# A one-core hybrid decoder layer: one weight split moved on two engines, and the order of the gated-embedding tail rewritten

## The chip, the core and the metric

The kernel runs on one NeuronCore of a Trainium2 chip. The metric is the time of one execution in microseconds (us) of device time; lower is better. TensorE does the matmuls into PSUM, VectorE and ScalarE the elementwise work, GpSimd one-column arithmetic and the transfers that add, and SyncE issues most other transfers.

## The reference

One decoder layer on 512 tokens of width 1024, in fp32: attention and a gated mixer, a squared-ReLU MLP, and at the end an input embedding `p` gated per layer. Only that last part, with the product in front of it, is touched:

```
gate = jax.nn.sigmoid(jnp.einsum('bsd,de->bse', h, w_ple_gate[i]) + b_ple_gate[i])
ple = jnp.einsum('bsp,pd->bsd', p[i], w_ple[i]) * gate
h = h + rms_norm(ple, ple_post_g[i])
```

`h` is 512 x 1024, `w_ple_gate` 1024 x 1024. `rms_norm` divides each token's row by the root of its mean square and multiplies by a gain row.

## The kernel before

Five instruction streams are written out by hand, one per engine, and tied by semaphores; each engine works through its stream strictly in order. An fp32 product is made from three matmuls: every operand is split into a high part, which ScalarE rounds off (a "hi" copy), and a low part, which VectorE subtracts (a "lo" split); TensorE then multiplies high by high, low by high, high by low (lines 2694, 2698, 2699). Tokens are handled in four tiles of 128 rows, t = 0 to 3.

**The gate product.** `h @ w_ple_gate` is cut into 2 x 2 blocks and made by seven block products (a Strassen scheme), each for two token tiles j = 0, 1. `GATE_PRODUCTS` gives TensorE's order: (0,0), (0,1), (1,0), (1,1), (2,0), (3,0), (2,1), (4,0), (3,1), (5,0), (4,1), (6,0), (5,1), (6,1), written (block, j); a product is 12 matmuls of 512 columns, and the last one is made in two halves of 256. The weights of the seven blocks are GATE_11, GATE_21, GATE_T1, GATE_T2, GATE_T3, GATE_T4, GATE_22. The T blocks are sums of weight blocks. GpSimd's queue makes them with adding transfers into `raw_second` or `raw` (`add_gate`, line 2467), in two parts each. A part of T4 is added to the same place as the same part of T2, so its transfer waits until VectorE's lo split of that part of T2 is done. In a split weight `gate_split_hi` (ACT L2120) reads the raw sum, then `gate_split_lo` (DVE L1355). The tokens' side needs the turned hidden state: TensorE turns a tile of `h` by four small matmuls per half (`turn_h2`, L2749) into PSUM bank 6 or 7, and ScalarE copies it out (`h2_copy_raw`, L2160, into `h2T_a` or `h2T_b`; `h2_split_hi`, L2166). There are eight such halves, i = 0 to 7, and halves 6 and 7 use the banks of halves 4 and 5. `seed_e` (L2198) writes the bias into two banks, `gate_copy` (L2209) copies a product's result to where it is added to. `h2_sum` (L1403) makes sums of blocks of the hidden state, which are split in the same way (L2182, L1408).

**The tail.** The gated rows are made in nine pieces (`GATE_TILES`): 0 = (t0, left), 1 = (t1, left), 2 = (t2, right), 3 = (t2, left), 4 = (t3, right), 5 = (t0, right), 6 = (t3, left), 7 and 8 = the two quarters of (t1, right). For each there is `sigmoid(i)` (ACT L2220, or L2217 for pieces 2 and 4), `gate_ple(i)`, a multiply with the embedding (DVE L1440), and `square_ple(i)`, which sums squares (ACT L1596). GpSimd adds a token tile's sums, one column each (L2506, L2517), takes the power -1/2 (L2519) and so gives the tile's `rstd`. Tiles are finished in the order 2, 0, 3, 1. For t = 2 and 0 (`ADDED_IN_OUT`) VectorE scales the gated rows by rstd and gain (L1464), and GpSimd issues an adding store into `out` (L2527), on top of `h`, which is stored there earlier. For t = 3 and 1 VectorE multiplies by the gain (`gain_ple`, L1452) and adds rstd times that to `h` (L1473), and SyncE stores each piece (L2679). For the very last piece, 8, GpSimd writes the root of the partial sum into an extra column beside the piece (L2510), so that the last square gives the whole sum. GpSimd's loop takes a whole tile at a time: partial sums, rstd, then the wait for VectorE's scaling and the adding store, and then the next tile.

Of the kernel before, what the change touches and what calls it, by code (L numbers as in the profile page):

```python
# [39 lines left out]
P = 128  # L40
D = 1024
# [274 lines left out]
def hymba_layer(nc, x, xT, pT, weights, columns, rope, ws, rows, out):  # L316
# [6 lines left out]
    with ExitStack() as ctx:  # L323
# [158 lines left out]
        ple_tmp = stat[:, 56:59]  # L482
# [260 lines left out]
        def _(dve):  # L743
# [712 lines left out]
            def add_ple(t):  # L1456

                tiles = gate_tiles_of(t)
                if t in ADDED_IN_OUT:
                    dve.wait_ge(pl_rstd, TOKENS_DONE.index(t) + 1)  # L1460
                    for i in tiles:
                        dve.wait_ge(pl_gated, i + 1)
                        cut = slice(GATE_TILES[i][1], GATE_TILES[i][1] + GATE_TILES[i][2])
                        nc.vector.scalar_tensor_tensor(out=ple_of(t)[:, cut], in0=acc[:, t, cut],  # L1464
                                                       scalar=rstd_pl[:, t:t + 1], in1=ple_gain[:, cut],
                                                       op0=ALU.mult, op1=ALU.mult).then_inc(out_ready, 1)
                    return
                gain_ple(tiles[-1])
                dve.wait_ge(pl_rstd, TOKENS_DONE.index(t) + 1)
                dve.wait_ge(pl_gained, GAINED.index(tiles[-1]) + 1)  # L1470
                for i in tiles:
                    cut = slice(GATE_TILES[i][1], GATE_TILES[i][1] + GATE_TILES[i][2])
                    nc.vector.scalar_tensor_tensor(out=h[:, t, cut], in0=ple_of(t)[:, cut],  # L1473
                                                   scalar=rstd_pl[:, t:t + 1], in1=h[:, t, cut],
                                                   op0=ALU.mult, op1=ALU.add).then_inc(out_ready, 1)
# [27 lines left out]
            gate_split_lo(GATE_T2, 1)  # L1503
# [3 lines left out]
            h2_sum_split_lo(OF_E, 0)  # L1507
            h2_sum_split_lo(OF_S2, 0)
# [26 lines left out]
            add_ple(2)  # L1535
# [15 lines left out]
        def _(act):  # L1551
# [702 lines left out]
            gate_split_hi(GATE_T2, 1)  # L2254
            seed_e(0)
            seed_e(1)
# [3 lines left out]
            h2_split_hi(5)  # L2260
            h2_sum_split_hi(OF_E, 0)
            h2_sum_split_hi(OF_S2, 0)
# [27 lines left out]
            for i in range(4, len(GATE_TILES)):  # L2290
                sigmoid(i)
                square_ple(i)
# [5 lines left out]
        def _(pool):  # L2298
# [201 lines left out]
            for n, t in enumerate(TOKENS_DONE):  # L2500
                *before, last_tile = gate_tiles_of(t)
                total = D * EPS
                for place_in_row, i in enumerate(before):
                    partial = ple_tmp[:, place_in_row:place_in_row + 1]
                    pool.wait_ge(pl_squared, i + 1)
                    after(nc.gpsimd.tensor_scalar(partial, ss_pl[:, i:i + 1], total, None, ALU.add))  # L2506
                    total = partial
                if last_tile == LAST_GATED:

                    nc.gpsimd.tensor_tensor(last_gated[:, width_of(LAST_GATED):], total, plus_half, ALU.pow  # L2510
                                            ).then_inc(root_ready, 1)
                    pool.wait_ge(pl_squared, last_tile + 1)
                    mean = ss_pl[:, last_tile:last_tile + 1]
                else:
                    pool.wait_ge(pl_squared, last_tile + 1)
# [759 lines left out]
```

## Time and profile before

| what | value |
|---|---|
| median of 3 runs (lowest, highest) | 585.18 us (585.04, 585.37) |
| the profiled execution's own time | 586.4 us |
| its span, first to last instruction | 584.7 us |
| granted TensorE clock, mean of the span | 0.991 of full speed |
| TensorE busy, share of the span | 97% |
| VectorE, ScalarE, GpSimd busy | 86%, 64%, 20% |

The profiled execution is one more execution than the three timed ones. Its span leaves out 1.7 us before the first and behind the last instruction. Rows of the trace give the start from the span's beginning in us, the duration, and in brackets how long the engine had been idle and what released it.

### The profile page before, as it was taken

The numbers are of one execution on the slowest core, as the hardware profiler recorded it, in microseconds if no ns is written. First come the engines' busy times: TensorE is split into PE (matmuls) and PEld (weight loads), VectorE is DVE, ScalarE is ACT, GpSimd is POOL, SyncE is SP. The second block draws the span as 40 slices with busy tenths as digits, with TensorE's granted clock in tenths as the row PEclk, the third lists the DMA queues.
The fourth block names the chain that finished last, engine by engine and source line by source line (L and its number), as shares of the span: only waits on it lengthen the run. The fifth ranks groups of instructions, "written<-read, shape, count | busy, mean of one in ns | idle before, by whom it ended". The sixth has DMA issues, their size and how long they took to land.

```text
span 584.7 us, 8927 instructions
## 1 busy us (share of the span) xinstructions
PE 569.1 (97%) x3364; PEld 496.0 (85%) x3364; DVE 501.1 (86%) x637; ACT 374.9 (64%) x595; POOL 114.2 (20%) x165
## 2 busy tenths in 40 slices
PE   9999999999999999999999999999999999999991
PEld 7888888888888888989999999999999999887881
DVE  5899895788676997999989999999899999787975
ACT  6886765785546646657665665666556655775862
POOL 0331536000104372101010011010100110123114
PEclk9999999999999999999999999999999999999996
DMA  8981008224003649377484592774754927877946
GB/s 270 372 309 62 0 5 321 73 72 143 3 1 109 243 173 298 78 228 188 89 256 106 143 253 44 246 161 90 242 121 112 281 40 214 242 234 141 288 128 140
DMA packets 28747, 95.30 MB, mean 163 GB/s; under 512 B 3232, under 2 KB 5664, under 8 KB 28320
## 3 DMA queue, kind: packets, MB, share of 16 engines
q1 hardware_dynamic: 20448, 67.64, 32.5%
q0 software_dynamic: 6672, 20.71, 20.6%
q10 hardware_dynamic: 1584, 6.37, 2.8%
q8 instruction: 27, 0.44, 0.3%
q14 instruction: 16, 0.13, 0.1%
HBM read 86.85 MB, written 7.34 MB: 161 GB/s over the span
## 4 chain that ended last, share of the span: by engine, by line
PE 77%; DVE 9%; DMA 6%; ACT 4%; POOL 2%; issue 2%; SPq 0%; DVEq 0%; ACTq 0%; POOLq 0%
PE psum L2694 24%; PE psum L2698 23%; PE psum L2699 23%; DMA ple_spill<-ple 2%; DVE up_lo L1078 2%; PE psum L2932 2%; DMA raw_second<-weights_dram 2%; PE psum L2912 1%; PE psum L2749 1%; DMA raw<-weights_dram 1%; ACT junk_late L1596 1%; DVE ple L1172 1%; DMA first_raw_a<-weights_dram 1%; PE psum L2763 1%; DVE t_lo L1223 1%
## 5 line engine op out<-in xcount | busy, mean ns | idle before, releaser
L2694 PE MATMUL psum<-t_hi,a_hi 128*128 128x512 f32 x216 | 85.0, 393 | 0.5 <-DVE acc L1282 0.5
L2698 PE MATMUL psum<-t_lo,a_hi 128*128 128x512 f32 x216 | 84.6, 392 | 0.0
L2699 PE MATMUL psum<-t_hi,a_lo 128*128 128x512 f32 x216 | 84.1, 389 | 0.0
L2694 PE MATMUL psum<-w_hi,actT_hi 128*128 128x512 f32 (+1 forms) x178 | 69.7, 392 | 0.0
L2699 PE MATMUL psum<-w_hi,actT_lo 128*128 128x512 f32 (+1 forms) x178 | 68.5, 385 | 0.0
L2698 PE MATMUL psum<-w_lo,actT_hi 128*128 128x512 f32 (+1 forms) x178 | 68.5, 385 | 0.0
L2698 PE MATMUL psum<-sum_lo,up_hi 128*128 128x256 f32 x224 | 63.4, 283 | 0.0
L2699 PE MATMUL psum<-sum_hi,up_lo 128*128 128x256 f32 x224 | 63.4, 283 | 0.0
L2694 PE MATMUL psum<-sum_hi,up_hi 128*128 128x256 f32 x224 | 63.2, 282 | 0.0
L2429 POOL DMA_DIRECT2D raw_x<-weights_dram x21 | 18.5, 882 | 216.1 <-DVE t_lo L1223 215.8
L2699 PE MATMUL psum<-actT_hi,up_lo 128*128 128x256 f32 (+1 forms) x200 | 60.0, 300 | 0.0
L2698 PE MATMUL psum<-actT_lo,up_hi 128*128 128x256 f32 (+1 forms) x200 | 60.0, 300 | 0.0
L2694 PE MATMUL psum<-actT_hi,up_hi 128*128 128x256 f32 (+1 forms) x200 | 59.9, 299 | 0.0
L1282 DVE TENSOR_TENSOR acc<-acc,psum 128x512 f32<-128x512 f32 x76 | 49.1, 681 | 1.8 <-PE psum L2699 1.8
L1078 DVE TENSOR_TENSOR up_lo<-raw,up_hi 128x1024 fp32r<-128x1024 f32 x37 | 46.8, 1264 | 2.6 <-ACT up_hi L1857 2.0
L2699 PEld LDWEIGHTS psum<-t_hi,a_lo 128*128 128x128 f32 x216 | 40.6, 188 | 8.9
L2694 PEld LDWEIGHTS psum<-t_hi,a_hi 128*128 128x128 f32 x216 | 40.7, 189 | 8.0 <-issue 0.8
L2698 PEld LDWEIGHTS psum<-t_lo,a_hi 128*128 128x128 f32 x216 | 40.7, 189 | 6.6
L2694 PEld LDWEIGHTS psum<-sum_hi,up_hi 128*128 128x128 f32 x224 | 42.9, 191 | 1.1
L2698 PEld LDWEIGHTS psum<-sum_lo,up_hi 128*128 128x128 f32 x224 | 42.9, 191 | 1.1
L2699 PEld LDWEIGHTS psum<-sum_hi,up_lo 128*128 128x128 f32 x224 | 42.9, 191 | 0.0
L2694 PEld LDWEIGHTS psum<-actT_hi,up_hi 128*128 128x128 f32 x200 | 38.2, 191 | 2.0
(298 smaller groups left out, 1453.7 us busy)
## 6 DMA issues: line engine op xcount, KB each, us to landing
raw<-weights_dram SPq DMA_DIRECT2D x40, 512.0 KB, 4.6
raw_o<-weights_dram SPq DMA_DIRECT2D x23, 512.0 KB, 4.4
raw_x<-weights_dram POOLq DMA_DIRECT2D x21, 512.0 KB, 5.5
raw_second<-weights_dram SPq DMA_DIRECT2D x16, 512.0 KB, 4.1
raw_x<-weights_dram SPq DMA_DIRECT2D x9, 512.0 KB, 6.2
qk_raw<-weights_dram SPq DMA_DIRECT2D x8, 512.0 KB, 6.7
raw_o<-weights_dram POOLq DMA_DIRECT2D x7, 512.0 KB, 6.9
raw_second<-weights_dram POOLq DMA_DIRECT2D x6, 512.0 KB, 7.7
```

The lines of the kernel that those rows point to most:

```text
L1078: nc.vector.tensor_tensor(up_lo[q % UP_SLOTS][:], block_source(step, j), up_hi[q % UP_SLOTS][:].bitcast(F32), ALU.subtract).then_inc(block ...
L1172: drained_by_dve(nc.vector.tensor_copy(ple[:, t, half * W:(half + 1) * W], psum[:, bank1["ple", i], :]), ("ple", i))
L1223: nc.vector.tensor_tensor(t_lo[n % T_RING][:], t_source(n), t_hi[n % T_RING][:].bitcast(F32), ALU.subtract).then_inc(t_lo_done, 1)
L1282: nc.vector.tensor_tensor(part, part, bank, how).then_inc(product_added, 1)
L1596: nc.scalar.activation(place_at[:, 0:source.shape[-1]], source, ACT.Square, scale=scale, accum_out=sums).then_inc(done, 1)
L2429: nc.gpsimd.dma_start(raw_x[step % 2][:], weights[down_in_stream(step, rows, half)], accum_op=ALU.add).then_inc(x_added, 16)
L2694: begin = nc.tensor.matmul(out, a_hi, b_hi, start=first, stop=False, skip_group_check=read_between)
L2698: nc.tensor.matmul(out, a_hi, b_lo, start=False, stop=False, skip_group_check=read_between)
L2699: return nc.tensor.matmul(out, a_lo, b_hi, start=False, stop=last, skip_group_check=read_between)
L2749: mm = nc.tensor.transpose(psum[:, banks[name], j * P:(j + 1) * P], source[:, j * P:(j + 1) * P], ident[:])
L2763: mm = nc.tensor.matmul(out, wsT[:, g, :], gv[:, :, g * GD:(g + 1) * GD], start=True, stop=True)
L2932: mm = nc.tensor.matmul(psum[s * DH:(s + 1) * DH, BANK_O, pair * P:(pair + 1) * P], v[:, k, head * DH:(head + 1) * DH], probsT_of[place_in ...
```

## The change

Nothing that is computed changes. (1) On ScalarE and VectorE the split of the second part of GATE_T2, which waits for an adding transfer, is moved behind the copies of the third token tile (t = 2, halves 4 and 5), the seeds and the first sum's split. (2) In the tail, ScalarE takes sigmoids 5, 6, 7 and 8 ahead of squares 4, 5, 6 and 7. (3) GpSimd makes the partial sums of squares as soon as a square is there, and the rstd of t = 3 ahead of the adding store of t = 0. (4) VectorE adds piece by piece, with the gains of pieces 6, 7 and 8 in other places. The scratch columns become one per tile, and SyncE's order of stores is written out with the same result for the pieces that it stores.

```diff
-        ple_tmp = stat[:, 56:59]
+        ple_partial, ple_mean = stat[:, 56:60], stat[:, 61:62]
...
             gate_split_lo(GATE_T2, 0)
-            gate_split_lo(GATE_T2, 1)
             h2_sum(OF_E, 0)
             h2_sum(OF_S2, 0)
             h2_sum(OF_S3, 0)
             h2_sum_split_lo(OF_E, 0)
+            gate_split_lo(GATE_T2, 1)
             h2_sum_split_lo(OF_S2, 0)
...
-            add_ple(2)
+            scale_ple(2)
             gate_ple(4)
             gate_ple(5)
             gain_ple(4)
-            add_ple(0)
+            scale_ple(0)
             gate_ple(6)
+            gain_ple(6)
             gate_ple(7)
-            add_ple(3)
             gain_ple(7)
+            add_ple(4)
             gate_ple(8)
+            add_ple(6)
+            gain_ple(8)
             add_ple(1)
+            add_ple(7)
+            add_ple(8)
...
             gate_copy(COPY_C11, 0)
-            gate_split_hi(GATE_T2, 1)
-            seed_e(0)
-            seed_e(1)
             gate_copy(COPY_C11, 1)
             h2_copy_raw(4)
             h2_copy_raw(5)
             h2_split_hi(5)
+            seed_e(0)
+            seed_e(1)
             h2_sum_split_hi(OF_E, 0)
+            gate_split_hi(GATE_T2, 1)
             h2_sum_split_hi(OF_S2, 0)
...
-            for i in range(4, len(GATE_TILES)):
-                sigmoid(i)
-                square_ple(i)
+            sigmoid(4)
+            sigmoid(5)
+            square_ple(4)
+            sigmoid(6)
+            square_ple(5)
+            sigmoid(7)
+            square_ple(6)
+            sigmoid(8)
+            square_ple(7)
+            square_ple(8)
...
+            partial_sum(0)
+            partial_sum(1)
+            partial_sum(2)
+            ple_rstd(2)
+            add_in_out(2)
+            partial_sum(4)
+            ple_rstd(0)
+            ple_rstd(3)
+            add_in_out(0)
+            partial_sum(7)
+            nc.gpsimd.tensor_tensor(last_gated[:, width_of(LAST_GATED):], ple_partial[:, 1:2], plus_half, ALU.pow
+                                    ).then_inc(root_ready, 1)
+            ple_rstd(1)
...
-            order = [i for t in TOKENS_DONE for i in gate_tiles_of(t)]
+            order = (2, 3, 0, 5, 4, 6, 1, 7, 8)
```

ScalarE's stream at the first place, before. `w_hi<-raw_second` is the split of T2's second part, `psum<-gate_bias_row` the two seeds, `h2T_b<-psum` the two copies of t = 2:

```order
L2209 ACTIVATE psum<-psum 128x512
L2120 ACTIVATE w_hi<-raw_second 128x1024
L2198 ACTIVATE psum<-gate_bias_row 128x512 x2
L2209 ACTIVATE psum<-psum 128x512
L2160 ACTIVATE h2T_b<-psum 128x4x128 x2
L2166 ACTIVATE actT_hi<-psum 128x4x128
L2182 ACTIVATE actT_hi<-gate_e 128x4x128
```

The same place with the change (three lines further down in the file):

```order
L2212 ACTIVATE psum<-psum 128x512 x2
L2163 ACTIVATE h2T_b<-psum 128x4x128 x2
L2169 ACTIVATE actT_hi<-psum 128x4x128
L2201 ACTIVATE psum<-gate_bias_row 128x512 x2
L2185 ACTIVATE actT_hi<-gate_e 128x4x128
L2123 ACTIVATE w_hi<-raw_second 128x1024
```

Seven instructions that stood behind the split now stand ahead of it.

GpSimd's stream at the end, before, from the adding store of t = 2 on. All of `stat<-stat` is one column wide; L2506 is a partial sum, L2517 the last addition of a tile, L2519 the power:

```order
L2527 DMA out_dram<-ple_late_b_147 128x1024
L2506 TENSOR_SCALAR stat_56<-stat_56 128x1
L2517 TENSOR_SCALAR stat_56<-stat_56 128x1
L2519 TENSOR_TENSOR stat_56<-stat_56 128x1
L2527 DMA out_dram<-ple_late_a_146 128x1024
L2506 TENSOR_SCALAR stat_56<-stat_56 128x1
L2517 TENSOR_SCALAR stat_56<-stat_56 128x1
L2519 TENSOR_TENSOR stat_56<-stat_56 128x1
L2506 TENSOR_SCALAR stat_56<-stat_56 128x1 x2
L2510 TENSOR_TENSOR last_gated_148<-stat_56 128x1
L2519 TENSOR_TENSOR stat_56<-stat_56 128x1
```

With the change the same stretch is (L2516, L2526, L2528, L2539 and L2551 answer to L2506, L2517, L2519, L2527 and L2510):

```order
L2539 DMA out_dram<-ple_late_b_147 128x1024
L2516 TENSOR_SCALAR stat_56<-stat_56 128x1
L2526 TENSOR_SCALAR stat_56<-stat_56 128x1
L2528 TENSOR_TENSOR stat_56<-stat_56 128x1
L2526 TENSOR_SCALAR stat_56<-stat_56 128x1
L2528 TENSOR_TENSOR stat_56<-stat_56 128x1
L2539 DMA out_dram<-ple_late_a_146 128x1024
L2516 TENSOR_SCALAR stat_56<-stat_56 128x1
L2551 TENSOR_TENSOR last_gated_148<-stat_56 128x1
L2528 TENSOR_TENSOR stat_56<-stat_56 128x1
```

The partial sum of piece 1 is gone from it (it now stands ahead of the first store), and the adding store of t = 0 has moved from ahead of t = 3's rstd to behind it.

## Rows read from the trace of the kernel before

**Rows 1.** The page's chain that ended last, by engine

```profile
PE 77%; DVE 9%; DMA 6%; ACT 4%; POOL 2%; issue 2%; SPq 0%; DVEq 0%; ACTq 0%; POOLq 0%
```

**Rows 2.** Timeline of TensorE: start, duration, engine line, operation, [idle before]

```profile
535.60 0.40 PE L2699 MATMUL psum<-w_hi,actT_lo 128*128 128x512 f32 x1
...
536.62 0.47 PE L2694 MATMUL psum<-w_hi,actT_hi 128*128 128x512 f32 x1
...
539.24 0.39 PE L2699 MATMUL psum<-w_hi,actT_lo 128*128 128x512 f32 x1
540.80 0.63 PE L2749 MATMUL psum<-ident,h 128*128 128x128 f32 x4 [1.17 <-ACT h2T_b L2160]
...
542.16 0.48 PE L2694 MATMUL psum<-w_hi,actT_hi 128*128 128x512 f32 x1
...
569.25 0.39 PE L2699 MATMUL psum<-w_hi,actT_lo 128*128 128x512 f32 x1
```

**Rows 3.** Timeline of ScalarE between 537 and 554 us

```profile
537.59 1.06 ACT L2120 ACTIVATE w_hi<-raw_second 128x1024 fp32r<-128x1024 f32 x1 [3.64 <-DMA raw_second<-weights_dram]
...
540.07 1.08 ACT L2160 ACTIVATE h2T_b<-psum 128x512 f32<-128x512 f32 x2
...
551.13 1.05 ACT L2120 ACTIVATE w_hi<-raw_second 128x1024 fp32r<-128x1024 f32 x1
...
553.36 0.60 ACT L2209 ACTIVATE acc<-psum 128x512 f32<-128x512 f32 x1 [0.65 <-PE psum L2699]
```

**Rows 4.** Timeline of GpSimd: the transfer of T4's second part is issued

```profile
540.21 0.86 POOL L2467 DMA_DIRECT2D raw_second<-weights_dram  x1 [2.20 <-DVE w_lo L1355]
```

**Rows 5.** DMA issues at 537.1, 540.0 and 540.2 us: size, us to landing

```profile
raw_second<-weights_dram POOLq DMA_DIRECT2D x1, 512.0 KB, 5.4
...
ple_late_a<-ple_spill SPq DMA_DIRECT2D x1, 1024.0 KB, 6.9
raw_second<-weights_dram POOLq DMA_DIRECT2D x1, 512.0 KB, 8.6
```

**Rows 6.** Timeline of ScalarE in the tail

```profile
570.11 0.63 ACT L1596 ACTIVATE junk_late<-acc 128x512 f32<-128x512 f32 x1 [0.76 <-DVE acc L1440]
...
570.74 0.58 ACT L2220 ACTIVATE acc<-psum 128x512 f32<-128x512 f32 x1
...
574.01 0.63 ACT L1596 ACTIVATE junk_late<-acc 128x512 f32<-128x512 f32 x1 [2.70 <-DVE acc L1440]
```

**Rows 7.** Timeline of VectorE in the tail

```profile
571.96 1.42 DVE L1464 SCALAR_TENSOR_TENSOR ple_late_a<-acc,stat,ple_gain 128x512 f32<-128x512 f32 x2 [1.28 <-POOL stat L2519]
573.29 0.69 DVE L1440 TENSOR_TENSOR acc<-acc,ple_late_b 128x512 f32<-128x512 f32 x1
...
575.38 0.68 DVE L1452 TENSOR_TENSOR ple_late_b<-acc,ple_gain 128x512 f32<-128x512 f32 x1
...
580.56 1.54 DVE L1473 SCALAR_TENSOR_TENSOR h<-ple_late_a,stat,h 128x512 f32<-128x512 f32 x3 [1.22 <-POOL stat L2519]
```

**Rows 8.** Timeline of GpSimd, one earlier power and the tail

```profile
525.79 1.53 POOL L2329 TENSOR_TENSOR stat<-stat 128x1 f32<-128x1 f32 x1
...
571.00 0.27 POOL L2517 TENSOR_SCALAR stat<-stat 128x1 f32<-128x1 f32 x1 [1.66 <-ACT junk_late L1596]
...
573.96 0.92 POOL L2527 DMA_DIRECT2D out_dram<-ple_late_a  x1 [2.03 <-DVE ple_late_a L1464]
574.61 0.56 POOL L2506 TENSOR_SCALAR stat<-stat 128x1 f32<-128x1 f32 x1
575.27 0.84 POOL L2517 TENSOR_SCALAR stat<-stat 128x1 f32<-128x1 f32 x1
576.20 0.57 POOL L2519 TENSOR_TENSOR stat<-stat 128x1 f32<-128x1 f32 x1
576.85 1.76 POOL L2506 TENSOR_SCALAR stat<-stat 128x1 f32<-128x1 f32 x2
578.70 0.61 POOL L2510 TENSOR_TENSOR last_gated<-stat 128x1 f32<-128x1 f32 x1
```

More of the change, by code:

```diff
@@ L1453, in gain_ple, with scale_ple, add_ple @@
                                         ).then_inc(pl_gained, 1)
[L1456 to L1468, printed above, removed]
+            def scale_ple(t):
                 dve.wait_ge(pl_rstd, TOKENS_DONE.index(t) + 1)
-                dve.wait_ge(pl_gained, GAINED.index(tiles[-1]) + 1)
-                for i in tiles:
+                for i in gate_tiles_of(t):
                     cut = slice(GATE_TILES[i][1], GATE_TILES[i][1] + GATE_TILES[i][2])
-                    nc.vector.scalar_tensor_tensor(out=h[:, t, cut], in0=ple_of(t)[:, cut],
-                                                   scalar=rstd_pl[:, t:t + 1], in1=h[:, t, cut],
-                                                   op0=ALU.mult, op1=ALU.add).then_inc(out_ready, 1)
+                    nc.vector.scalar_tensor_tensor(out=ple_of(t)[:, cut], in0=acc[:, t, cut],
+                                                   scalar=rstd_pl[:, t:t + 1], in1=ple_gain[:, cut],
+                                                   op0=ALU.mult, op1=ALU.mult).then_inc(out_ready, 1)
+            def add_ple(i):
+                t, c0, width = GATE_TILES[i]
+                cut = slice(c0, c0 + width)
+                dve.wait_ge(pl_rstd, TOKENS_DONE.index(t) + 1)
+                dve.wait_ge(pl_gained, GAINED.index(i) + 1)
+                nc.vector.scalar_tensor_tensor(out=h[:, t, cut], in0=ple_of(t)[:, cut],
+                                               scalar=rstd_pl[:, t:t + 1], in1=h[:, t, cut],
+                                               op0=ALU.mult, op1=ALU.add).then_inc(out_ready, 1)
             def tail_down(d):
@@ L2498, in _, with partial_sum, ple_rstd @@
             add_s4(1)
[L2500 to L2507, printed above, removed]
+            def partial_sum(i):
+                t = GATE_TILES[i][0]
+                partial = ple_partial[:, t:t + 1]
+                before = partial if i != gate_tiles_of(t)[0] else D * EPS
+                pool.wait_ge(pl_squared, i + 1)
+                after(nc.gpsimd.tensor_scalar(partial, ss_pl[:, i:i + 1], before, None, ALU.add))
+            def ple_rstd(t):
+                last_tile = gate_tiles_of(t)[-1]
+                mean = ple_mean
+                pool.wait_ge(pl_squared, last_tile + 1)
                 if last_tile == LAST_GATED:
-                    nc.gpsimd.tensor_tensor(last_gated[:, width_of(LAST_GATED):], total, plus_half, ALU.pow
-                                            ).then_inc(root_ready, 1)
-                    pool.wait_ge(pl_squared, last_tile + 1)
                     mean = ss_pl[:, last_tile:last_tile + 1]
                 else:
-                    pool.wait_ge(pl_squared, last_tile + 1)
-                    mean = ple_tmp[:, 2:3]
-                    after(nc.gpsimd.tensor_scalar(mean, ss_pl[:, last_tile:last_tile + 1], total,
+                    after(nc.gpsimd.tensor_scalar(mean, ss_pl[:, last_tile:last_tile + 1], ple_partial[:, t:t + 1],
                                                   1.0 / D, ALU.add, ALU.mult))
@@ L2520, in _, with add_in_out @@
                                         ).then_inc(pl_rstd, 1)
[L2521 to L2527 removed]
+                pool.wait_ge(pl_rstd, TOKENS_DONE.index(t) + 1)
+            def add_in_out(t):
+                n = ADDED_IN_OUT.index(t)
+                if n == 0:
+                    pool.wait_ge(late_added, s4_added)
+                    pool.wait_ge(stored, 16 * len(ADDED_IN_OUT))
+                pool.wait_ge(out_ready, 2 * (n + 1))
+                nc.gpsimd.dma_start(out[t * P:(t + 1) * P], ple_of(t), accum_op=ALU.add).then_inc(late_added, 16)
+            partial_sum(0)
[11 more added lines that the diff above has]
+            ple_rstd(1)
         @block.sync
```

7 lines of the change are left out of this document (removed).

## The prediction

> **What bounds the kernel now.** I read the chain of waits first, then the timelines of the stretches that the diff touches, then the transfers. The chain is TensorE for 77% of the span [rows 1], so the long middle of the program is a matmul stream that the change does not touch; what can move are the places where TensorE stands still, and the tail behind its last product. TensorE's timeline shows one hole [rows 2]: the last matmul of product (1,0) starts at 539.24, and the first of (1,1) only at 542.16, 2.92 us later. Between them lie the turnings of halves 6 and 7, and the first waits 1.17 us for ScalarE's copy of half 4. The turnings of halves 4 and 5, which waited for nothing, took from 535.60 to 536.62, 1.02 us. ScalarE's timeline says why its copy was late [rows 3]: it stood 3.64 us in front of the split of T2's second part, until that adding transfer landed at 537.6, and the copies, at 540.07, were queued behind the split and the seeds. From 542.16 on TensorE's rows show no further hole; it ends two half products (24 matmuls of 0.12 us) behind (5,1), at about 572.5. The tail is another chain: ScalarE, VectorE and GpSimd hand the last pieces round, and VectorE's last adds start at 580.56 [rows 7], 8 us after the last matmul.
>
> **Part 1, the moved split.** Half 4 is turned by the time product (1,0) begins, 536.62 [rows 2], and ScalarE is then free. The copies start there instead of at 540.07, and are done long before 539.24. The turnings of 6 and 7 then take the 1.02 us of the pair before: TensorE gains 2.92 - 1.02 = **1.90 us**. It keeps it only if nobody is late for one of its later products. What stands ahead of the split now is work of about 0.54 us each (two copies took 1.08 [rows 3]): six of them, from 536.6, end near 539.5 or a little later. So the split starts 1.9 us later than 537.59. Its own user, product (3,0), comes two products behind (1,1), at 2.7 us each (536.62 to 539.24 is eleven of twelve matmuls [rows 2]), so at about 545.7; VectorE's half of the split is done by 542, and nobody waits.
>
> Who else waits for that lo split? GpSimd's queue: the transfer of T4's second part is issued by it, at 540.21 [rows 4], and would go out at 542.1. It took 8.6 us [rows 5], so it lands at 550.7. ScalarE took it at 551.13 [rows 3], would want it 1.9 us earlier, at 549.2, and so now waits 1.5 us for it. Behind that split stood a copy that had waited 0.65 us for TensorE [rows 3]. From the landing, two operations (551.13 to 552.7 or so, then the wait) lead to this copy: 550.7 + 1.5 = 552.2 against 553.36. So the elementwise engines are only 1.15 us ahead from here, TensorE still 1.90. Behind this GpSimd's two adding transfers of 256 KB (S4) follow in the same queue; ScalarE wants them only behind that copy, a table load and two sigmoids, and I cost them at nothing, with that work as cover. If it is gone, each us beyond counts once. SyncE's load of the embedding waits for the same lo split; it takes 6.9 us [rows 5], lands near 549, and is wanted only by VectorE's first multiply of the tail, behind all of this.
>
> **Part 2, the tail.** TensorE's product (5,1) starts its last matmul at 569.25 - 1.90 = 567.35 and ends at 567.75. Sigmoid 6 no longer queues behind square 5: it ran at 570.74 [rows 6], and now runs at 567.8. Square 4, in front of it, is ahead by the elementwise lead of 1.15 us at least, and I take it to be out of the way. Square 5 follows at 568.3, against 570.11 [rows 6]: 1.8 us earlier. That is again TensorE's lead, and the elementwise lead of 1.15 no longer counts. From square 5 the steps are as before: 1.85 us to the scaling of t = 0 (570.11 to 571.96), which thus starts at 570.15; 1.33 us to the multiply of piece 6 (573.29), now 571.5; 0.72 us to its square (574.01), now 572.2. Only here does GpSimd's new order work. It takes the last addition for t = 3 right behind the square, 0.89 us after its start (570.11 to 571.00 [rows 6, 8]), at 573.1, where it started at 575.27. That addition took 0.27 us with VectorE waiting and 0.84 beside VectorE's multiply at 575.38, which ended at 576.06 as the addition ended at 576.11 [rows 7, 8]. VectorE is at work on pieces 6 and 7 at 573, so I bound it by 0.27 and 0.84 and take 0.7. The power starts 0.09 us later and takes 0.57: done at 574.0 to 574.6. The adding store of t = 0 now stands here. It needed up to 0.58 us between VectorE's end (573.38) and its start, and 0.65 us until GpSimd's next instruction (573.96 to 574.61). I charge 0.3 to 0.6 and 0.65: 575.0 to 575.8. Then one partial sum instead of two. The two took 1.85 us up to the root (576.85 to 578.70), 0.93 each; one beside an idle VectorE took 0.66 (574.61 to 575.27). That gives the root at 575.7 to 576.8. The early partial sums of pieces 0, 1, 2 and 4 lie in front of the stores, where GpSimd only waited for squares; what they cost if that cover is gone is 0.93 each. From the root to the last adds it is 580.56 - 578.70 = 1.86 us: 577.5 to 578.6. So the last adds come **3.0 to 1.9 us** earlier. The three adds and the last store behind them are the same. Since VectorE is busy beside most of these one-column steps, I lean to the dear end, 2.2 us.
>
> **The Trainium skill** (SBUF — State Buffer, section Who interferes with whom) says that a VectorE instruction with two SBUF inputs and a GpSimd instruction that reads SBUF exclude each other, and that whichever comes second is held until the first ends. The pair at 575.27 and 575.38 agrees, as both end together [rows 7, 8]. By that rule every one-column step moved beside a multiply costs what is left of the multiply, and the sum would be the dear end, 1.9 us.
>
> **Sum.** No instruction is added and one wait is taken away: 1.9 us from TensorE's hole, carried to square 5, and about 0.3 us net from GpSimd's order, 2.2 in all. The profiled execution took 586.4 us for a span of 584.7, 1.2 above the median of the runs; the saving is the same against either: 585.2 - 2.2 = **583.0 us**. A measurement of this kernel can tell about 0.2%, 1.2 us, from no change: below 584.0 is faster, above 586.4 slower.
>
> **Rivals.**
>
> (a) **The late transfer, in part.** T4's second part now starts together with the 1 MB load of the embedding, as before, but also sees the next weight load sooner. Until it lands at 551.2 the lead of TensorE hides it; each us later moves the end by one. If it takes 10 us instead of 8.6 (landing 552.1), 0.9 of the 2.2 is lost, 584.1. For it: the same queue took 5.4 us for the same size with nothing beside it and 8.6 with company [rows 5]. Against it: the company was there before too.
>
> (b) **The late transfer, in full: slower.** The gain is used up when it lands at 553.4, 11.3 us after its issue, and the loss reaches 0.2% at 12.5 us. If it were held until the 1 MB load is in (6.9) and then took 5.4, it would land at 554.4, and the time be 586.2; with 8.6 behind the 6.9 it would land at 557.6, and the time be 589.4. ScalarE's in-order stream would stand before the split, the copies behind it would be late, and TensorE would stop at product (4,1). I name 587.8, between the two. Against it: in the trace the two transfers were issued 0.2 us apart and both were under way together [rows 5].
>
> The Trainium skill (DMA: Bandwidth & Descriptors, section Queues, rings and completion order) says that each transfer engine takes turns between its queue rows, packet by packet; by this the transfer is slowed and not held back, which is case (a) at most. The 8.6 beside the 6.9 agrees.
>
> (c) **GpSimd and VectorE in each other's way.** One power took 1.53 us beside VectorE at 525.79, against 0.57 [rows 8]. If the root, now beside VectorE's adds, takes that (0.92 more than its 0.61) and the store's issue 0.3 more, 1.2 of the 2.2 is lost: 584.2. By the skill's rule just named the root can be held by one multiply and add of at most 0.75 us, which makes this price the ceiling. For it: VectorE has less idle time in the new tail. Against it: the root of before already stood beside VectorE and took 0.61.
>
> (d) **The hole stays.** If something else holds the turnings of halves 6 and 7, or TensorE loses its lead again at a later product, only the tail's order is left. It is worth 0 to 0.8 us, since what it takes from the last stretch (one partial sum, 0.9) it pays back as the store's 0.95: 584.8. This is the case in which the main edit does not do what it says. Against it: the releaser shown at the first turning is ScalarE's copy [rows 2].
>
> **How the numbers follow.** Forecast 0.68, (a) 0.10, (b) 0.05, (c) 0.12, (d) 0.05. The forecast's own range is 582.1 (3.0 saved, and 0.1) to 583.8 (0.6 short of the 2.2, and 0.2). For 8 in 10 I go from 582.1 up over (a), (c) and (d) to 585.0; left out are (b) and the outer ends of the others. Faster takes the forecast and half or a little less of (a) and (c): 0.77. Same takes the rest of (a) and (c), and (d): 0.18. Slower is (b): 0.05.
>
> **What would show it.** Right: matmuls of (1,1) start near 540.3 instead of 542.16, and product (5,1) ends near 567.7; ScalarE waits for `raw_second` near 550, not for `raw_second` at 537; GpSimd's power for t = 3 stands ahead of the store of t = 0 and starts near 573.7; the last adds start between 577.5 and 578.7. Wrong: TensorE shows a hole before product (4,1) (a or b), one-column steps of over 0.9 us in the tail (c), or a hole of over 1 us still before 542 (d). The span should be near 582.5.

## The result, and the profile after

The changed kernel takes **593.0 us** (median of 4 runs, 592.65 to 593.65), the kernel before 585.27 us (4 runs on the same chip, 585.04 to 585.86): a ratio of 1.0132, 95% interval 1.0114 to 1.0149. It is 7.7 us slower, where 2.2 us of gain were forecast. The profiled execution took 593.34 us with a span of 591.6 us, 6.9 more than before.

The page of the kernel after, the chain that ended last by engine, and TensorE's busy time: DMA has fallen to 3% and VectorE to 1%, and TensorE's share has grown from 77 to 92% [rows 1], although it is idle more.

```profile
PE 570.8 (96%) x3364; PEld 498.4 (84%) x3364; DVE 500.9 (85%) x637; ACT 375.1 (63%) x595; POOL 113.8 (19%) x165
...
PE 92%; DMA 3%; ACT 2%; DVE 1%; POOL 1%; issue 1%; DVEq 0%; ACTq 0%; POOLq 0%
```

TensorE's timeline of the kernel after (start, duration, engine line, operation, idle before and its releaser):

```profile
538.53 0.39 PE L2725 MATMUL psum<-w_hi,actT_lo 128*128 128x512 f32 x1
538.76 1.03 PE L2775 MATMUL psum<-ident,h 128*128 128x128 f32 x8
539.55 0.48 PE L2720 MATMUL psum<-w_hi,actT_hi 128*128 128x512 f32 x1
...
558.46 0.39 PE L2725 MATMUL psum<-w_hi,actT_lo 128*128 128x512 f32 x1
566.01 0.76 PE L2720 MATMUL psum<-w_hi,actT_hi 128*128 128x512 f32 x1 [7.16 <-ACT acc L2212]
...
569.56 0.63 PE L2725 MATMUL psum<-w_hi,actT_lo 128*128 128x512 f32 x1
...
578.97 0.28 PE L2725 MATMUL psum<-w_hi,actT_lo 128*128 128x256 f32 x1
```

The hole that the edit aimed at is gone: product (1,0) starts its last matmul at 538.53 and (1,1) its first at 539.55, 1.02 us later instead of 2.92 [rows 2]. A new hole of 7.16 us stands at 558.85, in front of product (4,1). ScalarE, same kernel:

```profile
550.35 1.06 ACT L2123 ACTIVATE w_hi<-raw_second 128x1024 fp32r<-128x1024 f32 x1 [1.74 <-DMA raw_second<-weights_dram]
...
551.83 0.58 ACT L2212 ACTIVATE acc<-psum 128x512 f32<-128x512 f32 x1
...
553.72 1.09 ACT L2223 ACTIVATE acc<-psum 128x512 f32<-128x512 f32 x2
561.82 0.63 ACT L2185 ACTIVATE actT_hi<-h2T_a 128x512 fp32r<-128x512 f32 x1 [7.01 <-DMA h2T_a<-gate_s]
```

ScalarE takes T4's second part as forecast (the wait of 1.74 against "1.5"). Then it is done with the two sigmoids at 554.81 and stands 7.01 us until S4's second adding transfer lands. (The split of S4's first half waits on one semaphore that counts both transfers; the first had landed at 556.8.) The kernel before took the same instruction at 556.24 with no wait:

```profile
556.24 0.63 ACT L2182 ACTIVATE actT_hi<-h2T_a 128x512 fp32r<-128x512 f32 x1
```

Product (4,1) itself does not read S4. It waits for the bank that ScalarE's `gate_copy` empties (`acc` L2212, 565.29 to 565.86), and in ScalarE's order this copy stands behind both splits of S4, both of GATE_22 and a sigmoid. S4's own products, (6,0) and (6,1), come later. A copy moved ahead of the splits of S4 would have let (4,1) run, and (6,0) would have been the first to wait; this was not run.

Which transfers were under way says why S4 was late. GpSimd's and SyncE's issues, before:

```profile
543.21 1.32 POOL L2476 DMA_DIRECT2D h2T_a<-gate_s  x1 [2.15 <-DVE h2T_b L1403]
548.04 1.27 POOL L2476 DMA_DIRECT2D h2T_a<-gate_s  x1 [3.52 <-DVE gate_s L1403]
...
550.21 0.70 SPq L2667 DMA_DIRECT2D ple_late_b<-ple_spill  x1
550.95 0.51 SPq L2668 DMA_DIRECT2D ple_gain<-row_gate_dram  x1
551.50 0.92 SPq L2671 DMA_DIRECT2D out_dram<-h  x2
```

And after:

```profile
541.49 0.86 POOL L2477 DMA_DIRECT2D raw_second<-weights_dram  x1 [4.21 <-DVE w_lo L1355]
542.05 1.64 POOL L2486 DMA_DIRECT2D h2T_a<-gate_s  x1
545.43 1.27 POOL L2486 DMA_DIRECT2D h2T_a<-gate_s  x1 [1.74 <-DVE gate_s L1403]
...
547.60 0.49 SPq L2693 DMA_DIRECT2D ple_late_b<-ple_spill  x1
548.13 0.45 SPq L2694 DMA_DIRECT2D ple_gain<-row_gate_dram  x1
548.62 0.95 SPq L2697 DMA_DIRECT2D out_dram<-h  x2
```

Upstream this execution ran 0.72 us ahead of the one before. With that taken off, T4's part went out 2.0 us later (540.21 to 541.49) and the second half of the embedding 1.9 us earlier (550.21 to 547.60), since the two weight loads ahead of it in SyncE's queue wait for VectorE's lo splits of GATE_T3 (the second started at 548.60 before and at 545.99 now), which no longer stand behind the late split of T2. The two closed up by 3.9 us. S4's two transfers were not issued later (543.21 to 542.05 and 548.04 to 545.43), but the first now stands directly behind T4's part in GpSimd's queue. The transfers issued between 540 and 562 us (size, median us from issue to landing), before and then after:

```profile
ple_late_b<-ple_spill SPq DMA_DIRECT2D x1, 1024.0 KB, 6.7
...
h2T_a<-gate_s POOLq DMA_DIRECT2D x2, 256.0 KB, 6.7
```

```profile
ple_late_b<-ple_spill SPq DMA_DIRECT2D x1, 1024.0 KB, 9.0
out_dram<-h SPq DMA_DIRECT2D x2, 512.0 KB, 11.8
raw_second<-weights_dram POOLq DMA_DIRECT2D x1, 512.0 KB, 8.8
h2T_a<-gate_s POOLq DMA_DIRECT2D x2, 256.0 KB, 15.5
```

S4's two transfers took 8.4 and 5.0 us before (mean 6.7) and now 14.7 and 16.4 (mean 15.5); the second lands at 561.8 instead of 553.0. The stretches of the kernel after (us, then busy us and count by engine, granted clock, DMA share, GB/s) show the transfer engines full between 550 and 560 us, at 342 GB/s (before, the same stretch had a DMA share of 1.07 and 330 GB/s):

```profile
core 0: us, PE busy (x) PEld busy (x) DVE busy (x) ACT busy (x) POOL busy (x), PEclk, DMA share, GB/s
550.00:560.00 10.00, 8.85 (x40) 6.98 (x38) 3.63 (x5) 4.43 (x6) 0.00 (x0) 1.00 1.14 342
560.00:570.00 10.00, 3.99 (x10) 3.16 (x11) 7.04 (x11) 6.78 (x14) 0.46 (x2) 0.66 0.10 30
```

The second row has a cost of its own: the granted clock of the stretch is 0.66 (0.50 between 566 and 570 us), and the first nine matmuls behind the hole run 0.43 us apart instead of 0.23. The 36 matmuls of 512 columns from the hole to the last halves took 10.20 us (566.01 to 576.21), and 8.16 in the kernel before: 2.04 us more.

The tail after, GpSimd and then VectorE's last adds:

```profile
582.04 0.65 POOL L2528 TENSOR_TENSOR stat<-stat 128x1 f32<-128x1 f32 x1
582.99 0.92 POOL L2539 DMA_DIRECT2D out_dram<-ple_late_a  x1 [0.30 <-POOL stat L2528]
583.66 1.24 POOL L2516 TENSOR_SCALAR stat<-stat 128x1 f32<-128x1 f32 x1
584.98 0.56 POOL L2551 TENSOR_TENSOR last_gated<-stat 128x1 f32<-128x1 f32 x1
...
586.79 1.54 DVE L1471 SCALAR_TENSOR_TENSOR h<-ple_late_a,stat,h 128x512 f32<-128x512 f32 x3 [1.97 <-POOL stat L2528]
```

From the start of the last matmul to the last adds it is 7.82 us; before it was 8.33 (572.23 to 580.56 [rows 7]), so 0.51 is won. From the last adds to the end of the span it is 4.8 us, before 4.1: 0.7 is lost. The stores issued from 575 us on, after:

```profile
out_dram<-h SPq DMA_DIRECT2D x3, 256.0 KB, 4.9
out_dram<-ple_late_a POOLq DMA_DIRECT2D x1, 512.0 KB, 6.2
out_dram<-h SPq DMA_DIRECT2D x2, 128.0 KB, 2.6
```

Before, these were 2.7, 5.4 and 2.1 us. The 4.9 is the middle of three: the two stores of t = 3, issued before the last adds, took 4.9 and 5.2 us (before 2.7 each), and the one behind the last adds 2.5 (before 2.0). What ends the span is the very last store of 128 KB: 2.8 us against 2.0.

**The balance of the spans.** Upstream -0.72; first hole -1.90; new hole with its restart +7.32 (558.46 to 566.01 is 7.55, less the 0.23 of a step); lower clock +2.04; tail to the last adds -0.51; end +0.7. The sum is +6.9, the difference of the spans.

### The profile page after: what moved, and what is told of

Read it like the earlier page. It is cut to its first block, busy times and chain, and to the rows that moved or that the text cites. A ratio compares the mean times of both kernels' runs of the same rounds, so it can differ in the third digit from the quotient of the medians.

```text
span 591.6 us, 8928 instructions
## 1 busy us (share of the span) xinstructions
PE 570.8 (96%) x3364; PEld 498.4 (84%) x3364; DVE 500.9 (85%) x637; ACT 375.1 (63%) x595; POOL 113.8 (19%) x165
## 4 chain that ended last, share of the span: by engine, by line
PE 92%; DMA 3%; ACT 2%; DVE 1%; POOL 1%; issue 1%; DVEq 0%; ACTq 0%; POOLq 0%
PE psum L2720 29%; PE psum L2724 28%; PE psum L2725 28%; DMA h2T_a<-gate_s 3%; PE psum L2775 2%; PE psum L2958 2%; PE psum L2938 1%; PE psum L2829 1%; PE psum L2789 1%; ACT w_hi L2123 1%; DVE w_lo L1355 0%; PE psum L2812 0%; ACT junk_late L1599 0%; POOL stat L2528 0%; DVE ple_late_a L1461 0%
## 5 line engine op out<-in xcount | busy, mean ns | idle before, releaser
L2720 PEld LDWEIGHTS psum<-w_hi,actT_hi 128*128 128x128 f32 x178 | 34.0, 191 | 14.2 <-DVE w_lo L1355 7.6
```

The lines of the kernel that those rows point to most:

```text
L2720: begin = nc.tensor.matmul(out, a_hi, b_hi, start=first, stop=False, skip_group_check=read_between)
```

## The experiments

Theories: **A, crowding**: S4's adding transfers come late because SyncE's plain transfers, those that do not add (the embedding's second half, the gain row, two stores of `h`; 2.5 MB) now share the transfer engines with them. **B, GpSimd's own queue**: they come late because GpSimd issues them close behind T4's part (0.56 us after it instead of 3.0), whatever SyncE does. **C, the new tail** costs the time. **D, lateness**: T4's part, issued 2 us later, is the cost by itself. All times below are medians, with the kernel before run on the same chip: 586.06 us for the first four, 586.05 for the next four, 586.10 for the last two.

### e1_part1: the moved split alone

The kernel before with part (1) of the diff only; tail as before.

```diff
             gate_split_lo(GATE_T2, 0)
-            gate_split_lo(GATE_T2, 1)
...
             h2_sum_split_lo(OF_E, 0)
+            gate_split_lo(GATE_T2, 1)
```

> Only the moved split, with the tail of the kernel before. Theory A (crowding: the split moved back sends GpSimd's adding transfers of T4 and S4 2 us later and SyncE's loads and stores 2 us earlier, so that the S4 transfers are served among 3 MB of plain ones): the whole loss is here, S4 lands near 561 to 562, TensorE stands some 7 us, 592 to 594 us. Theory B (GpSimd's own queue: the second S4 transfer suffers because T4's and both S4's are issued close behind each other): the same loss here. Rival C (the new tail order costs the time): 583 to 585 us here.

Measured: 592.27 us, ratio 1.0103 (1.0080 to 1.0125). TensorE's hole and the transfers:

```profile
565.78 0.76 PE L2694 MATMUL psum<-w_hi,actT_hi 128*128 128x512 f32 x1 [7.21 <-ACT acc L2209]
```

```profile
raw_second<-weights_dram POOLq DMA_DIRECT2D x1, 512.0 KB, 8.9
h2T_a<-gate_s POOLq DMA_DIRECT2D x2, 256.0 KB, 15.5
```

The moved split alone gives 592.27 us, the whole change 593.0 (ratios 1.0103 and 1.0132, with intervals that overlap): nearly all of the loss comes with it. C falls as its cause.

### e2_tail: the tail alone

The changed kernel with part (1) undone.

```diff
             gate_split_lo(GATE_T2, 0)
+            gate_split_lo(GATE_T2, 1)
...
             h2_sum_split_lo(OF_E, 0)
-            gate_split_lo(GATE_T2, 1)
```

> Only the new order of the tail, with the split of T2's second part where it was. Theories A and B: nothing is late, 584.4 to 585.3 us (0 to 0.8 saved, from the prediction's case d). Rival C: 590 us or more.

Measured: 585.47 us, ratio 0.9989 (0.9974 to 1.0003): no difference that can be told. S4's transfers took 7.1 us. The tail shows both its sides: last matmul to last adds 7.81 us (before 8.33), but the stores and a partial sum are dearer:

```profile
575.89 1.23 POOL L2516 TENSOR_SCALAR stat<-stat 128x1 f32<-128x1 f32 x1
```

```profile
out_dram<-h SPq DMA_DIRECT2D x3, 256.0 KB, 5.0
out_dram<-ple_late_a POOLq DMA_DIRECT2D x1, 512.0 KB, 5.8
```

### e3_held: SyncE's transfers held until S4 is in

```diff
+            sp.wait_ge(late_added, s4_added)
             sp.dma_start(ple_late[1][:], ple_spill[:, 2:4, :]).then_inc(ple_loaded[1], 16)
```

> The changed kernel, with SyncE's second load of the embedding, the gain row and the two stores of h held until both S4 transfers have landed. Theory A: S4 lands at 553 to 555 as the trace of before has it, TensorE has no hole before its last product, 582.5 to 584.5 us. Theory B: the queue of GpSimd is as before the hold, so S4 stays near 560 and the time near 592, or above, since the held loads then come too late as well.

Measured: 584.81 us, ratio 0.9982 (0.9967 to 0.9997). GpSimd issues as in the kernel after (T4's part at 541.76, S4's at 542.32 and 545.70), yet they land in time:

```profile
raw_second<-weights_dram POOLq DMA_DIRECT2D x1, 512.0 KB, 9.1
h2T_a<-gate_s POOLq DMA_DIRECT2D x2, 256.0 KB, 10.6
```

```profile
555.38 0.33 SPq L2694 DMA_DIRECT2D ple_late_b<-ple_spill  x1
```

```profile
559.58 0.47 PE L2721 MATMUL psum<-w_hi,actT_hi 128*128 128x512 f32 x1 [0.47 <-ACT acc L2212]
```

One wait on SyncE takes back 1.5% by the two ratios (1.0132 and 0.9982), some 8.8 us, and leaves 0.47 of the 7.16 us hole. B falls as the cause of the loss: the same issues, 0.56 us apart, now take 10.6 us in the mean. That is still 3.9 us more than in the kernel before, so closer issues or the earlier weight loads may lengthen the transfers as well, by an amount that the cover just hides. D falls as the sole cause: T4's part is as late as in the changed kernel (ScalarE waits 2.00 us for it).

### e4_early: only the two stores of `h` taken out of the crowd

The changed kernel with SyncE's two stores of `h` ahead of the load of the embedding's first half, instead of behind the gain row.

```diff
+            for t in ADDED_IN_OUT:
+                sp.wait_ge(h2_ready, t + 1)
+                sp.dma_start(out[t * P:(t + 1) * P], h[:, t, :]).then_inc(stored, 16)
             sp.wait_ge(filled, filled2["down", 7])
...
             sp.dma_start(ple_gain[:], rows["gate"][:, 1, :]).then_inc(post_loaded, 16)
-            for t in ADDED_IN_OUT:
-                sp.wait_ge(h2_ready, t + 1)
-                sp.dma_start(out[t * P:(t + 1) * P], h[:, t, :]).then_inc(stored, 16)
```

> The changed kernel, with the two stores of h (1 MB in all) issued before SyncE's load of the embedding, as soon as h is ready, when the transfer engines are half idle. Theory A: 1 MB of the 3 MB of company is gone from the time of S4; at 350 GB/s that is 3 us, S4 lands near 558 to 559, 589 to 591 us. Theory B: no change, 592.5 to 593.5 us.

Measured: 590.86 us, ratio 1.0082 (1.0060 to 1.0104). The hole is 4.38 us, S4's second transfer 13.6 us instead of 16.4. Taking 1 MB of the 2.5 MB out of the crowd shortens it by 2.8 us and the hole by as much (7.16 to 4.38); the rest is crowd enough.

### e5_crowd_before: the crowd brought into the kernel before

No split is moved. SyncE issues the embedding's second half, the gain row and the two stores ahead of the last weight load.

```diff
             gate_x(GATE_22, 0)
-            gate_x(GATE_22, 1)
             sp.dma_start(ple_late[1][:], ple_spill[:, 2:4, :]).then_inc(ple_loaded[1], 16)
...
                 sp.dma_start(out[t * P:(t + 1) * P], h[:, t, :]).then_inc(stored, 16)
+            gate_x(GATE_22, 1)
```

> The kernel before, all splits and the tail as they were; only SyncE's queue is reordered: the second load of the embedding, the gain row and the two stores of h (3 MB in all counted with the 0.5 MB row) are issued ahead of the last weight load, near 546 instead of 550. Theory A (crowding by plain transfers): S4, which landed at 551.6 and 553.0, now lands near 560, TensorE gets a hole of 4 to 7 us at the products behind it, 589 to 592 us. Rival D (what matters is that T4's second part is issued late, which it is not here): 585 to 586 us.

Measured: 589.78 us, ratio 1.0069 (1.0054 to 1.0085). TensorE and the transfers:

```profile
563.51 0.76 PE L2694 MATMUL psum<-w_hi,actT_hi 128*128 128x512 f32 x1 [4.47 <-ACT acc L2209]
```

```profile
out_dram<-h SPq DMA_DIRECT2D x2, 512.0 KB, 12.1
h2T_a<-gate_s POOLq DMA_DIRECT2D x2, 256.0 KB, 13.9
```

S4's transfers were issued 3.0 us behind T4's part and 4.8 us apart, as in the kernel before, and still took 13.9 us. Crowding without any late split makes a hole at the same product. It is smaller (4.47 against 7.16 us), and the crowd is not placed as in the changed kernel: it begins at 543.48, 2.1 us ahead of S4's second transfer, where there it begins 2.2 us behind it. (It has 2.5 MB, not the 3 of the text above. The last weight load, now behind it, took 12.1 us and landed at 559.5, before ScalarE came to it at about 560.8, so it isn't what holds TensorE.) The first hole is missing in this execution, because the adding transfer of T2's second part happened to take 7.7 us (527.40 to 535.13) and not 9.3 (528.24 to 537.59); T4's part was thus issued sooner, at 537.75, and the loss came all the same. That shows A without lateness: a crowd of plain transfers is enough to make S4 late.

### e6_mid: the split half as far back

ScalarE's split stands ahead of the seeds, and VectorE's ahead of the third sum and of the first sum's lo split (the diff shows ScalarE's part), so that T4's part goes out at 539.97 (after: 541.49).

```diff
             h2_split_hi(5)
+            gate_split_hi(GATE_T2, 1)
             seed_e(0)
             seed_e(1)
             h2_sum_split_hi(OF_E, 0)
-            gate_split_hi(GATE_T2, 1)
```

> The changed kernel with T2's second split between the copies of t = 2 and the seeds, so that it starts when its transfer lands (about 538) and T4's second part is issued at about 540.5 instead of 542.2, while everything else keeps its 2 us. Theory A: S4 gains 1.6 us of free queue but still meets SyncE's loads from 547 on, lands near 557 to 560, 588 to 591 us. Rival D: T4's part is on time, so S4 lands by 554, 583 to 584 us.

Measured: 585.68 us (583.73 to 587.66, the widest spread of all), ratio 0.9993 (0.9980 to 1.0007). SyncE's crowd starts at 547.37, as early as in the kernel after, but S4's transfers took 10.4 and 9.7 us and TensorE's hole is 0.19 us. T4's part goes through the same queue ahead of S4's. Here it landed at 548.6, 1.2 us into the crowd; in the kernel after at 550.3, 2.7 us into it. A's figure was missed: T4's part and S4's first transfer, both issued 1.5 us earlier, made most of the difference, so the issue time counts once the crowd is there. I read this as both being needed: plain transfers early, and adding ones still queued behind each other when they come (in e5 the crowd began at 543.5, while T4's part, issued at 537.75, and S4's first were under way). That is argued from single executions, and the profiled one of e6 took 584.55 us, 1.1 less than its median, so a usual run may have more of a hole. The spread of e6's own runs would fit a kernel that stands near the edge.

### e7_midheld: both

e6_mid with e3's wait on SyncE.

```diff
             gate_x(GATE_22, 1)
+            sp.wait_ge(late_added, s4_added)
             sp.dma_start(ple_late[1][:], ple_spill[:, 2:4, :]).then_inc(ple_loaded[1], 16)
```

> e6 with SyncE's second load of the embedding and all behind it held until S4 has landed. Theory A: S4 lands near 553 to 554, TensorE keeps its 1.9 us, ScalarE waits under 1 us for T4, 583 to 584.5 us. If the two are both needed, e7 is 0.3 to 0.8 us below e3.

Measured: 584.13 us (583.79 to 584.80), ratio 0.9969 (0.9958 to 0.9979): 1.8 us faster than before by the ratio. TensorE shows no hole from 539 us on, and the last adds start at 577.72. That is 2.84 us earlier than in the kernel before, 2.42 after the 0.42 by which this execution was ahead upstream (its transfer for T2's second part went out at 536.68 instead of 537.10).

### e8_tailx: early stores and another order on VectorE

e7_midheld with e4's early stores, and VectorE's multiply and gain of piece 6 ahead of the scaling of t = 0.

```diff
-            scale_ple(0)
             gate_ple(6)
             gain_ple(6)
+            scale_ple(0)
```

> e7 with the two stores of h issued early as in e4, and VectorE's multiply and gain of piece 6 moved ahead of the scaling of t = 0, where VectorE had stood idle 1.9 us. The square of piece 6, and with it rstd of t = 3 and the root, come about 2 to 3 us earlier; the adding store of t = 0 then ends about together with the last plain store. 580.5 to 582.5 us. If the tail is bound by something else (TensorE's end, the adding store), 583 to 584 us as e7.

Measured: 582.30 us (582.21 to 582.76), ratio 0.9941 (0.9927 to 0.9954). With the multiply of piece 6 no longer behind the scaling, the last adds start at 575.96, 6.20 us after the last matmul instead of 7.81. What the early stores add by themselves wasn't run; up to the last matmul they gain nothing that the traces show (569.76 against 569.91 in e7, with 0.17 of it upstream).

### e9_store_first: the adding store of t = 0 where it was

e7_midheld with one swap on GpSimd.

```diff
             ple_rstd(0)
-            ple_rstd(3)
             add_in_out(0)
+            ple_rstd(3)
```

> The split in between and the hold as in e7_midheld (584.13 us, last adds to end of span 4.8 us), but GpSimd issues the adding store of t = 0 ahead of the rstd of t = 3, as the kernel before does. Theory (the end crowded by the adding store): the store goes out near 571.5 while GpSimd only waits for the square of piece 6, so it lands before the last plain stores are issued; these take 2.7 us and less again instead of 4.9 to 5.2, last adds to end of span is 4.1 us, and the time is 583.4 us, 0.7 less than e7. Rival (the 0.7 us at the end is not the store's): plain stores stay over 4 us, the time stays at 584.1. Second rival (the store delays the rstd of t = 3): the power for t = 3 starts more than 0.5 us later than 572.98, and the time is 584.1 or more.

Measured: 582.66 us (582.40 to 583.26), ratio 0.9940 (0.9926 to 0.9953). GpSimd in the tail:

```profile
571.40 0.92 POOL L2539 DMA_DIRECT2D out_dram<-ple_late_a  x1 [2.03 <-DVE ple_late_a L1461]
572.29 0.35 POOL L2526 TENSOR_SCALAR stat<-stat 128x1 f32<-128x1 f32 x1
572.73 0.64 POOL L2528 TENSOR_TENSOR stat<-stat 128x1 f32<-128x1 f32 x1
```

From the last adds to the end it is 4.1 us again (576.82 to 580.9), against 4.8 in e7. The very last store takes 2.0 us, against 2.7 in e7. The two stores of t = 3 take 3.2 us each, not the 2.7 expected (e7: 3.3 and 5.2). And the last adds come 0.6 us sooner after the last matmul (7.19 against 7.81). The store costs nothing there, since GpSimd only waited for a square. So moving this store behind the rstd of t = 3 costs 1.3 us by these pieces (1.7 by the two ratios), about twice the 0.7 expected of it. With e8 it is one of two versions that beat both kernels, by 0.6%; the two together weren't run.

### e10_part1_held: the moved split with its cover, old tail

The kernel of e1_part1 with e3's wait.

```diff
+            sp.wait_ge(late_added, s4_added)
             sp.dma_start(ple_late[1][:], ple_spill[:, 2:4, :]).then_inc(ple_loaded[1], 16)
```

> Only the moved split, in the kernel before, with SyncE's load of the embedding's second half held until S4's adding transfers are in; the old tail. Theory (part 1 was right but for the crowding): S4's second transfer takes 10 us instead of 16.4, TensorE shows a hole of at most 0.6 us before product (4,1), the first hole stays gone, and of the 1.9 us about 1.4 are kept: 584.6 us, the same as e3_held (584.81) since the new tail is worth nothing net. If the new tail costs or saves by itself, the two differ by more than 0.5 us. Rival (the late T4 transfer itself is the cost): 587 us or more.

Measured: 585.50 us (585.14 to 586.58), ratio 0.9988 (0.9979 to 0.9998); 0.9 us more than the theory's figure. The wait works as in e3 (hole 0.51 us, S4 10.7 us). The last matmul starts at 570.34, 1.89 us earlier than in the kernel before, but the tail follows by less. The square of piece 5:

```profile
568.97 0.63 ACT L1596 ACTIVATE junk_late<-acc 128x512 f32<-128x512 f32 x1 [0.76 <-DVE acc L1440]
```

It is 1.14 us earlier than at 570.11 [rows 6], 0.77 of which is upstream (536.33 against 537.10). The same 0.77 is in TensorE's 1.89, of which 1.12 remain; the tail gets 0.37 of them. In the old order square 5 stands behind a chain of ScalarE and VectorE (sigmoid 5 behind square 4, square 4 behind the multiply of piece 4, that one behind the scaling of t = 2), and these two engines had waited 1.65 us for T4's part and 0.45 for S4. In e3_held they wait too (2.00 us for T4's part), but sigmoids 5 and 6 stand ahead: square 4 is 0.37 us earlier once more, square 5 1.08 and the last adds 1.64 (568.55 and 578.44, less 0.48 upstream). So two things hold back the tail of e10, the waits and the old order. Of the 1.27 us that the new tail thus gains at the last adds the end takes back 0.7, and by the ratios (0.9982 and 0.9988) no difference can be told.

## Why the prediction was wrong

**The step that failed** is in part 1: "GpSimd's two adding transfers of 256 KB (S4) follow in the same queue; ... I cost them at nothing, with that work as cover. If it is gone, each us beyond counts once." The cover was 3.2 us thick (553.0 to 556.24). I moved the queue by 1.9 us and left the transfers' own length alone. But they went from 6.7 to 15.5 us, as SyncE's queue was pulled forward by the same change that pushed GpSimd's back. I had followed SyncE's load of the embedding's first half, and not the 2.5 MB behind it, whose issue depends on an engine that now ran ahead. The hole of 7.16 us and the 2.04 of lower clock behind it make 9.2 us; between the forecast (2.2 less) and the spans (6.9 more) lie 9.1. That the two agree so well is in part luck: the 0.72 us upstream and the 0.7 at the end, neither of them forecast, cancel. Why a crowd lengthens an adding transfer so much more than a plain one stays open.

**Rivals.** (b) had the right sign, place and chain: an adding transfer late, ScalarE in order behind it, TensorE stopping at product (4,1). It had the wrong transfer: T4's part took 8.8 us (forecast 8.6) and was taken at 550.35. With its condition ("11.3 us after its issue") applied to S4's transfers the case held. The Trainium skill's rule that I set against it (DMA: Bandwidth & Descriptors, section Queues, rings and completion order: turns between queue rows, packet by packet) did not exclude it. The rows of S4 speak neither for nor against turns as such, but they show how slow an adding transfer can be beside a full queue: 5.0 us where the plain transfers joined late, 16.4 where four of them stood in SyncE's queue for most of the time. I had read "slowed and not held back" as "not slowed enough to matter". (a) did not happen: T4's wait of 1.74 us stayed covered. (d) did not happen.

**Part 1's other terms.** TensorE's first hole: 1.90 us forecast, 1.90 measured. ScalarE's wait for T4's part: 1.5 forecast, 1.74 measured. The lead of the elementwise engines at the copy behind it: 1.15 forecast, 0.81 measured (553.36 to 551.83, less 0.72 upstream). "It keeps it only if nobody is late" was the condition that failed. That TensorE's lead is what counts at square 5, "and the elementwise lead of 1.15 no longer counts", held where ScalarE and VectorE waited for no transfer. In e7, where ScalarE waits for neither T4 nor S4, square 5 came 1.84 us earlier (567.85, less 0.42 upstream; 1.8 forecast) and the last adds 2.42; the 2.2 taken for that point was sound. In e3, with the waits and the new order, square 5 got 1.08 us, and in e10, with the waits and the old order, 0.37.

"The saving is the same against either" (the profiled execution or the median) is doubtful too. The first hole hangs on when T2's adding transfer lands, and that differs between executions of the same instructions: 9.3 us in the kernel before and 8.8 to 9.4 in e1, e2, e3, e6 and e10, but 7.1 to 7.7 in the kernel after, e5, e7 and e9. The profiled execution, 1.2 us above the median of three (0.3 above the 586.1 of the later and larger sets), had a late one, and was 0.4 to 1.0 us behind all the others upstream (537.10 against 536.11 to 536.68). So in some executions the hole is likely smaller than 2.92 or, as in e5, absent, and the mean gain to be had from it is below 1.90. The runs of the kernel before spread from 584.63 to 587.71, those of e7 from 583.79 to 584.80, which would fit; this was not tested by itself.

**Part 2.** The order of the tail was worth 0.51 us at the last adds, near the 0.3 net forecast. The term "the three adds and the last store behind them are the same" failed: with the adding store issued at 582.99, 0.6 us ahead of the stores of t = 3, these took 4.9 and 5.2 instead of 2.7 us, the very last store 2.8 instead of 2.0, and the end 0.7 us longer. Net, the tail alone was worth nothing measurable (e2). e9 shows what the store's new place cost: 0.6 us at the last adds, less than the 0.95 to 1.25 that "0.3 to 0.6 and 0.65" charge for it, and 0.7 at the end, which was put at nothing.

**Rival (c)** happened in small: the partial sum of piece 7, beside VectorE's adds, took 1.24 us where 0.93 had been charged. The root took 0.56, so the 0.92 more feared for it did not come (in e9 it took 0.92 in all). By the Trainium skill's rule (SBUF — State Buffer, section Who interferes with whom) the second comer waits until the other's instruction ends. The rows bear out half of it. The partial sum ends at 584.90, 0.09 us behind a VectorE multiply with two SBUF inputs (584.39 to 584.81), so the two do seem to exclude each other. But by the starts GpSimd came first, 583.66 against 583.73, and it is GpSimd that took longer; VectorE's add took its usual 0.75. The pair that the prediction read as agreeing is of the same kind: the addition started at 575.27, ahead of the multiply at 575.38, and took 0.84, the multiply its usual 0.68. Starts on GpSimd are rough in a profile, so this settles nothing about who waits.

## What to carry to other kernels

When an edit moves work so that one queue's transfers go out later, follow every other queue too: what waits for an engine that now runs ahead is issued earlier, and the two can meet. Give a transfer that is hidden now a price for the new company, not only a new start, above all an adding one. A wait that holds back transfers nobody needs yet can be worth more than the edit that it protects (here 1.5% against 0.2 to 0.3%, e3 and e7), and the last adding store did best where its engine idled, well ahead of the last plain stores (e9). Ask also what stands behind a wait in an engine's order: TensorE stopped here for a copy that doesn't use the late transfer.

## What was unexpected

- An adding transfer of 256 KB took 5.0 and 8.4 us in the kernel before, 8.6 to 11.6 with SyncE's plain ones held back (e3, e7), and 13.6 to 16.4 in the crowd (after, e4, e5), but 9.7 and 10.4 in e6, where the queue went out 1.5 us earlier. The plain ones lengthened less (1 MB: 6.7 to 9.0 us), and the moved bytes per second between 550 and 560 us did not fall (342 GB/s, before 330).
- An adding transfer of 512 KB, issued at the same place behind the same instructions, took 7.1 to 9.4 us in different executions.
- A TensorE hole of 7.16 us cost 2.04 us more behind its end, with a granted clock of 0.50 between 566 and 570 us: nine matmuls of 512 columns 0.43 us apart, the pace of the lower level (1.2 GHz), then 0.23 again, that of 2.4 GHz. The price does not follow the hole's length alone: it was 2.84 us behind 7.21 in e1, 2.19 behind 4.47 in e5 and 1.53 behind 4.38 in e4 (36 matmuls in 11.00, 10.35 and 9.69 us, 8.16 before). The hole of 0.47 us in e3 left the clock alone: the matmuls behind it took their usual 0.39.
- A store of 256 KB took 2.7 us in the kernel before. With an adding store of 512 KB issued just ahead of it in the new tail, the first such store took 2.5 to 5.1 us in different runs (e6, e2), and the second, about 1 us later, 5.0 to 5.2 (after, e2, e3, e6, e7).
